# Layer 1 MLP with five deferred products and two weight sums on engines, two sums by DMA in layer 0

## The reference

```python
def _sq_relu_mlp(h, w1, w2):
    return jnp.square(jax.nn.relu(h @ w1)) @ w2
...
sh1, sc1, g1, sh2, sc2, g2 = jnp.split((silu_c @ ada_w[i] + ada_b[i])[:, None, :], 6, axis=-1)
...
h_lat = h_lat + g2 * _sq_relu_mlp(_modulate(_rms_norm(h_lat, norm2_g[i]), sh2, sc2), mlp_w1[i], mlp_w2[i])
```

## Time and profile before

| what | value |
|---|---|
| median of 3 runs | 2533.49 us |
| profiled execution | 2538.97 us |
| its span | 2537.4 us |
| TensorE matmul busy | 2310.9 us, 91% of the span |
| VectorE, ScalarE, GpSimd busy | 1748.4, 1148.5, 1150.7 us |
| mean granted TensorE clock | 0.960 of full speed |

### The profile page before, as it was taken

One profiled execution on the slowest core, in us unless ns is written; L12 is line 12 of the kernel. 1 busy time (PEld: TensorE's weight loads), 2 busy tenths in 40 slices (PEclk: granted clock), 3 DMA queues, 4 the chain that ended last, 5 costly groups with the idle time before them and its releaser, 6 DMA issues. The chain is left out here.

```text
span 2537.4 us, 38440 instructions
## 1 busy us (share of the span) xinstructions
PE 2310.9 (91%) x11430; PEld 1898.4 (75%) x11430; DVE 1748.4 (69%) x2843; ACT 1148.5 (45%) x2117; POOL 1150.7 (45%) x958
## 2 busy tenths in 40 slices
PE   5989989999999998999959979897988999999999
PEld 3768768788878787888848767775866777777777
DVE  5643886666666667666766478885378777787777
ACT  5544443333333333333344368886344545454554
POOL 0004533333433333334455657675644555465554
PEclk9999999999999999999969989999999999999999
DMA  7434325555555555444532211112311332322322
GB/s 267 166 133 166 101 54 145 148 153 137 144 135 143 140 147 136 132 132 132 141 111 83 100 57 34 34 44 113 112 46 46 100 95 91 91 91 87 99 87 95
DMA packets 132200, 283.55 MB, mean 112 GB/s; under 512 B 11408, under 2 KB 19984, under 8 KB 128784
## 3 DMA queue, kind: packets, MB, share of 16 engines
q1 hardware_dynamic: 111776, 242.09, 28.8%
q0 software_dynamic: 17408, 33.56, 7.9%
q10 hardware_dynamic: 2928, 6.82, 0.7%
HBM read 265.64 MB, written 83.89 MB: 138 GB/s over the span
## 5 line engine op out<-in xcount | busy, mean ns | idle before, releaser
L881 POOL TENSOR_TENSOR ht<-ht,l_side 128x512 f32<-128x512 f32 x112 | 147.6, 1318 | 401.1 <-ACT l_side L1020 397.2
L51 PE MATMUL l_z_ps<-nh,l_w1h 128*128 128x512 f32 (+1 forms) x816 | 292.9, 359 | 6.5 <-POOL l_w1l L58 3.4
L53 PE MATMUL l_z_ps<-nh,l_w1l 128*128 128x512 f32 (+1 forms) x816 | 291.7, 357 | 0.0
L52 PE MATMUL l_z_ps<-nl,l_w1h 128*128 128x512 f32 (+1 forms) x800 | 285.8, 357 | 0.0
L1324 DVE SCALAR_TENSOR_TENSOR ht<-l_yy_ps,mod,ht 128x512 f32<-128x512 f32 x336 | 236.4, 744 | 31.1 <-PE l_yy_ps L1640 29.9
L58 POOL TENSOR_TENSOR l_w1l<-early,l_w1h 128x512 fp32r<-128x512 f32 x104 | 136.4, 1318 | 190.0 <-ACT l_w1h L2189 190.0
L2754 PE MATMUL l_yy_ps<-l_ah,l_w2h 128*128 128x512 f32 x448 | 185.6, 414 | 22.2 <-DVE ht L2545 19.5
L1638 PE MATMUL l_yy_ps<-l_ah,l_w2h 128*128 128x512 f32 x448 | 191.2, 427 | 9.0 <-DVE ht L1324 9.0
L2081 POOL TENSOR_TENSOR ht<-ht,l_side 128x512 f32<-128x512 f32 x112 | 155.8, 1391 | 88.8 <-ACT l_side L2239 87.9
L3483 POOL TENSOR_TENSOR sc<-sc,den 128x640 f32<-128x640 f32 (+1 forms) x128 | 149.5, 1200 | 92.0 <-DVE den L3565 92.0
L1639 PE MATMUL l_yy_ps<-l_al,l_w2h 128*128 128x512 f32 x448 | 187.9, 420 | 0.0
(11 more groups left out here) (338 smaller groups left out, 6606.5 us busy)
## 6 DMA issues: line engine op xcount, KB each, us to landing
l_aw<-ada SPq DMA_DIRECT2D x128, 256.0 KB, 3.6
sums<-w SPq DMA_DIRECT2D x64, 512.0 KB, 7.4
maw<-ada SPq DMA_DIRECT2D x24, 1024.0 KB, 5.2
l_w1f<-w SPq DMA_DIRECT2D x32, 512.0 KB, 4.1
l_w2f<-w SPq DMA_DIRECT2D x32, 512.0 KB, 4.2
sums<-w POOLq DMA_DIRECT2D x32, 512.0 KB, 10.3
sums<-sums POOLq DMA_DIRECT2D x32, 512.0 KB, 6.1
l_w2f<-sums SPq DMA_DIRECT2D x64, 256.0 KB, 2.7
```

The lines of the kernel that those rows point to most:

```text
L51: pe.matmul(out, lh, rh, start=first, stop=False)
L52: pe.matmul(out, lh, rl, start=False, stop=False)
L53: return pe.matmul(out, ll, rh, start=False, stop=last)
```

## The change

In layer 0:

- `sums` keeps only S1 and S3 of w1 and w2. `start_sums` issues two copies a pair instead of four, and stands on SyncE's queue behind steps 2 to 7 instead of at the start of the pair. GpSimd issues two accumulating DMAs a pair instead of four (`add_sums`): one after M1's side add and the low parts behind it, the other at the end of the pair. Nothing is added on top of a sum any more.

In layer 1, from pair 2 on:

- S2 and S4 are formed in SBUF: for w1 by GpSimd (`sum1`, two additions a pair), for w2 by VectorE (`sum2`, two a pair). The loads of these four blocks go away (10 loads of 256 KB a pair instead of 14), the load slots and their order change.
- The low part of W2's S2 moves from VectorE to GpSimd, and the square of B21 from VectorE to ScalarE (`square_last`). B21's square now stands in an SBUF slot instead of PSUM, so M1 waits for the ReLU of B21, and M5 for the low part of T3.
- Five products are deferred instead of four. TensorE's order: M1, P2', M5, P3', M6, P4', M2, P5', M7, M3, P6', M4, P0, P1.
- The orders of ScalarE, VectorE, GpSimd and SyncE follow. Pairs 0 and 1 of layer 1, which use the plain product for the hidden layer, get the same sums for w2 and the new place of B21's square.

The diff, cut to its core:

```diff
-                    sp.dma_start(sums[0, 0:2, to]..., w1[1, one, :, :, 0:KC // 2]...).then_inc(s_sc, 16)
-                    sp.dma_start(sums[0, 2:4, to]..., w1[1, one, 0]...).then_inc(s_sc, 16)
-                    sp.dma_start(sums[1, 0:2, to]..., w2[1, two, :, :]...).then_inc(s_sc, 16)
-                    sp.dma_start(sums[1, 2:4, to]..., w2[1, chunks, :, 0:512]...).then_inc(s_sc, 16)
+                        sp.wait_ge(s_sums, p * 32)
+                    sp.dma_start(sums[0, :, to]..., w1[1, one, :, :, 0:KC // 2]...).then_inc(s_sc, 16)
+                    sp.dma_start(sums[1, :, to]..., w2[1, two, :, :]...).then_inc(s_sc, 16)
 
                 def pair(r, row, rows, first):
-                    if C:
-                        start_sums(r)
                     load1(r + 1, row(r + 1), 0)
                     if C and not first:
                         for k in range(2, STEPS):
                             load_a(r, row(r), k)
+                    if C:
+                        start_sums(r)
                     load1(r + 1, row(r + 1), 1)
...
                 def outputs(p, more):
-                    if C:
-                        if type(p) is not int or p:
-                            more_sums(p - 1, "S4")
-                        first_sums(p)
                     add(p, "M5")
...
                                 low1(p + 1, 1 if C else 0)
+                            if C:
+                                add_sums(p, 0)
...
                     if C:
-                        more_sums(p, "S2")
+                        add_sums(p, 1)
...
-                    more_sums(PAIRS - 1, "S4")
-                    pool.wait_ge(s_s4, 16 * PAIRS)
+                    pool.wait_ge(s_sums, 32 * PAIRS)
...
+                def sum1(p, i):
+                    a, b = (0, 1) if i == 2 else (2, 0)
+                    ...
+                    pool.tensor_tensor(w1f[:, a], w1f[:, a], w1f[:, b], ALU.add).then_inc(s_w1s, 1)
...
+                def square_last(p):
+                    act.wait_ge(s_rl, relu_at(p, "B21"))
+                    act.activation(inner("B21"), slot[RELU_SLOT["B21"]][:], ACT.Square).then_inc(s_sqa, 1)
...
                 def pair(p, earlier=True):    (VectorE)
                     if earlier:
                         pair_start(p)
-                    low2(p, 1)
-                    if earlier:
-                        acc(p - 1, 5)
-                    low2(p, 0)
                     zsum(p, "B11")
+                    if earlier:
+                        acc(p - 1, 5, (0,))
                     square(p, "B11")
+                    if earlier:
+                        acc(p - 1, 5, (1, 2, 3))
+                    low2(p, 0)
+                    sum2(p, 1)
                     zsum(p, "B22")
-                    low(p, "B11")
                     square(p, "B22")
                     zsum(p, "B12")
+                    if earlier:
+                        acc(p - 1, 6, (0,))
                     square(p, "B12")
+                    if earlier:
+                        acc(p - 1, 6, (1, 2, 3))
+                    low(p, "B11")
                     diff(p, "T1")
                     diff(p, "T2")
-                    if earlier:
-                        acc(p - 1, 6, (0, 1))
-                    square(p, "B21")
-                    if earlier:
-                        acc(p - 1, 6, (2, 3))
+                    diff(p, "T3")
                     low(p, "T2")
                     acc(p, 0, (0,))
-                    diff(p, "T3")
+                    low(p, "T3")
                     acc(p, 0, (1, 2, 3))
-                    low(p, "T3")
                     diff(p, "T4")
-                    acc(p, 1, (0, 1))
-                    low(p, "B21")
-                    acc(p, 1, (2, 3))
-                    low(p, "T4")
-                    acc(p, 2)
+                    acc(p, 1)
...
                 def pair(p, more, earlier=True):    (ScalarE)
...
+                    high(p, "B11")
+                    if earlier:
+                        side_read(p - 1, 6)
+                    high2(p, 2)
+                    high(p, "T2")
                     relu(p, "B21")
                     if more:
                         high1(p + 1, 0)
-                    high(p, "T2")
-                    if earlier:
-                        side_read(p - 1, 6)
+                    square_last(p)
                     high(p, "T3")
-                    high2(p, 2)
                     side_read(p, 0)
...
                 def pair(p, earlier=True):    (TensorE)
-                    for k, prod in enumerate(Z_ORDER):
+                    behind = {"M1": 2, "M5": 3, "M6": 4, "M2": 5, "M3": 6}
+                    for prod in Z_ORDER:
                         hidden(p, prod)
-                        if earlier and k < 3:
-                            product(p - 1, 3 + k)
-                    if earlier:
-                        product(p - 1, 6)
-                    for i in (0, 1, 2):
+                        if earlier and prod in behind:
+                            product(p - 1, behind[prod])
+                    for i in range(DEFERRED):
                         product(p, i)
```

More of the change, by code:

```diff
@@ L70, in sem @@
             return s
-        s_sums = [ctx.enter_context(nc.semaphore(n)) for n in ("sums13", "sums2", "sums4")]
+        s_sums = ctx.enter_context(nc.semaphore("sums"))
         def recycle_semaphores():
@@ L1891, in zsum_at, with after_square, summed1, summed2 @@
             return p * 3 + (PRE - 3 * PLAIN + ZSUMS.index(name) + 1)
-        def square_at(p, name):
-            order = Z_PLAIN[p] if is_plain(p) else SQUARES
-            return p * 4 + (PRE + order.index(name) + 1)
+        def after_square(eng, p, name):
+            if name == "B21":
+                eng.wait_ge(s_sqa, p + (PRE + 1))
+            else:
+                order = [n for n in Z_PLAIN[p] if n != "B21"] if is_plain(p) else SQUARES
+                eng.wait_ge(s_sqd, p * 3 + (PRE + order.index(name) + 1))
+        def summed1(eng, p, i):
+            eng.wait_ge(s_w1s, p * 2 + (PRE - 2 * PLAIN + W1_SUMS[i]))
+        def summed2(eng, p, i):
+            eng.wait_ge(s_w2s, p * 2 + (PRE + W2_SUMS[i]))
         def relu_at(p, name):
@@ L2174, in high1 @@
                 def high1(p, i):
-                    loaded1(act, p, i)
+                    if not is_plain(p) and i in W1_SUMS:
+                        summed1(act, p, i)
+                    else:
+                        loaded1(act, p, i)
                     if is_plain(p):
@@ L2228, in high @@
                             act.wait_ge(s_y, y_at(p - back, j, 3))
-                    if name == "B21":
-                        act.wait_ge(s_t, t_at(p, "T4"))
                     act.activation(operand(name)[0], inner(name), ACT.Copy).then_inc(s_ah, 1)
@@ L2348, in _ @@
                 relu(0, "B21")
+                square_last(0)
                 relu(0, "B12")
@@ L2409, in _ @@
                 pair(last, False)
+                side_read(last, 2)
                 high2(last, 6)
@@ L2558, in plain_rest @@
                     acc(p, 1, (0, 1))
+                    low(p, "T4")
+                    acc(p, 1, (2, 3))
                     low(p, "B21")
-                    acc(p, 1, (2, 3))
-                    low(p, "T4")
                     low(p, "T1")
@@ L2565, in plain_rest @@
                     low2(p, 6)
+                    sum2(p, 5)
                     acc(p, 3)
@@ L2579, in pair_start @@
                 def pair_start(p):
+                    low(p - 1, "T4")
+                    low(p - 1, "B21")
                     low(p - 1, "T1")
+                    acc(p - 1, 2)
+                    low(p - 1, "B22")
+                    low2(p - 1, 6)
+                    sum2(p - 1, 5)
                     acc(p - 1, 3)
-                    low2(p - 1, 6)
-                    low(p - 1, "B22")
                     low2(p - 1, 5)
@@ L2652, in _ @@
                 low(0, "B11")
-                square(0, "B21")
                 square(0, "B12")
-                diff(0, "T1")
                 square(0, "B22")
                 plain_rest(0)
-                low2(1, 1)
                 low2(1, 0)
+                sum2(1, 1)
                 square(1, "B11")
@@ L2804, in _ @@
                 pair(PAIRS - 1)
-                product(PAIRS - 1, 3)
+                for i in (2, 3):
+                    product(PAIRS - 1, i)
                 for n in range(3):
```

273 lines of the change are left out of this document (143 added, 130 removed).

## The result

| | median | runs | ratio to the kernel before | profiled execution | its span |
|---|---|---|---|---|---|
| before | 2533.56 us | 4 (2530.75 to 2535.92) | | 2538.97 us | 2537.4 us |
| after | 2434.24 us | 4 (2432.33 to 2434.94) | 0.9607, 95% interval 0.9591 to 0.9624 | 2434.44 us | 2432.9 us |

The median fell by 99 us, 3.9%; the forecast was 2428 with a range of 2408 to 2462. Between the spans of the two profiled executions the gain is 104.5 us, where the sum said 105.

The account below looks back on a forecast made before the run. TensorE was taken to bound both layers' MLPs, with layer 0 losing idle time and clock to late `ada_w` loads. Terms -90 - 5 - 6 - 6 + 2 = -105 from 2533.5 gave 2428 us, range 2408 to 2462.

Parts of the forecast that it names:

- The pauses: Layer 0's MLP pairs: all 14 TensorE stops before the last modulation step go, worth -90 us.
- (a): Sizing layer 0's pauses by pair length: 59.9 less 53.5 us, times 14 pairs, gives 90 us.
- (b): Sizing layer 0's pauses by 54.2 us idle plus 37 to 45 us of slow clock: 91 to 99 us.
- true control: Layer 0's last pair, copies behind the loads: VectorE waits only 0.63 us, steps 6 and 7 14.9 us after step 0.
- Last pair and tail: End of layer 0: late side adds in the last pair go, -5 us; one DMA fewer to await, -6 us.
- Layer 1, loop: Layer 1's 13 loop pairs: loss at bank read-outs falls from 1.5 to 1.0 us a pair, -6 us.
- Layer 1, outside the loop: Layer 1's pairs 0 and 1 and its very end: added sums on VectorE cost +2 us, bounds -2 and +5.
- VectorE and GpSimd on SBUF: Layer 1's new sums contend on shared SBUF interfaces: two `sum2` cost 2.4 us instead of 1.4, beside TensorE in the loop.
- (A): Rival, layer 0: pauses only shrink as accumulations run into the next pair's loads; +45 us, 2473; chance 9%.
- (B): Rival, layer 0: loads or VectorE's steps are late for another reason, so pauses stay; 2519 us; chance 3%.
- (C): Rival, layer 1: P1 waits longer as ScalarE and VectorE lock together; 2488 or 2448 us; chance above 2450 7%.
- (D): Rival, layer 1: GpSimd's 20 operations a pair set the pace; 2577 us at 2.5 us each; chance 2%.

Follow-up runs that it names:

- e2: The changed kernel with its two copies and two accumulations a pair put back at the old place at the pair's start: 2426.96 us, ratio 0.9559.
- e3: The kernel before with all four copies and four accumulating DMAs a pair at the new place, layer 1 as before: 2457.33 us, ratio 0.9692.
- e5: e2 with GpSimd issuing its two accumulations only after step 1 of the pair, so both lie beside the loads: 2452.74 us.
- e4: The kernel before with only layer 1's part of the change, layer 0 as before: 2537.2 us, ratio 1.0.
- e6: The changed kernel with GpSimd's wait for the last accumulations at layer 0's end moved to SyncE, ahead of layer 1's second-product weight loads: 2435.26 us.
- e7: The changed kernel with all VectorE read-outs of the first deferred product ahead of T3's low part in layer 1's pairs: 2420.23 us, ratio 0.9524.
- e9: The changed kernel run once more, unedited, in later rounds: 2434.85 us, ratio 0.9593.
- e1: The kernel before, unchanged, profiled a second time: median 2537.49 us, profiled execution 2537.39 us.

## Why the prediction was right, point by point

**The pauses (-90).** 91.8 measured, all 14 gone, pairs of 53.35 where 53.5 was worked out, the clock at 1.00, steps 6 and 7 14.9 us after step 0 (673.70 less 658.78). Both ways of sizing them held: (a), from pair lengths, to within 2 us, and (b), idle time plus slow clock, is 54.2 + 37.7 = 91.9 when the second part is taken from the matmuls' busy time. The last pair was a true control.

**What took them away.** The prediction names place and number together and read the earlier trace rows as three accumulations that happen to be issued there. e2, e3 and e5 correct this. Two sums at the old place have no pause, and two beside the loads have. The wait of 10.09 us in the first row made the place: it held S1 and S3 back into the time of the loads. The text had that number and used it only to say when S2 was issued. It had no effect on the forecast, as the pairs alone gain 75 us in e3 and 92 in e2, but it hid that the new place costs 6 us at the end.

**Last pair and tail (-5, -6).** 9.6 of 11. The tail was mis-sized by 1: the earlier trace rows have 6.1 us from S2's issue to S4's and 7.1 from there to the next stage; S2's wait is what goes, so 6.1 and not 7.1. Accordingly GpSimd's last issue to the next stage is 7.3 us, where 6 was said. This stretch also scatters by 2.5 us in the same code (64.1 and, in e4, 61.6). The forecast kept one DMA there as unavoidable; e2 shows it isn't, and e6 that taking the wait away doesn't help.

**Layer 1, loop (-6).** -4.2 over 12 pairs (0.34 a pair where 0.5 was said). The term that was mis-sized is the loss in P1: 1.07 us in place of 1.0, and 1.4 before in place of 1.5 (40.05 and 39.71 less 38.64). The mechanism was that of the text, and e7 shows that one moved line is worth three times what the deferral brought.

**Layer 1, outside the loop (+2, bounds -2 and +5).** It came out at +2, but by luck: both parts were wrong and cancel. From P1 of the last pair to the end it is +4.2 (34.3 less 30.1), where 1 to 2 was said for the end. Three low parts stand on VectorE ahead of the first read-out, two of them at 1.4 us. The first pairs, which were to lose a little, gained 2.2 in this trace, within their own scatter of 4. Also left out: B21's square now stands in SBUF, so the difference for T4 has both inputs there and takes 1641 ns in place of 678. It hides behind TensorE in the loop. Together layer 1 gave 2.1 of the 4 us; what is missing is the loop's. No timing here can tell 2.1 from nothing (e4). Its worth to this change is that it makes S2 and S4 unnecessary in layer 0.

**VectorE and GpSimd on SBUF.** The sums were priced at 1212 ns from the low parts; the two `sum2` have a mean of 1242 ns in the loop of the kernel after. That mean hides two durations. The group of the loop, and the two sums of one pair in order of time:

```profile
L2533 DVE TENSOR_TENSOR l_w2f<-l_w2f 128x512 f32<-128x512 f32 x20 | 24.8, 1242 | 0.3
```

```profile
1934.87 1.79 DVE L2533 TENSOR_TENSOR l_w2f<-l_w2f 128x512 f32<-128x512 f32 x1
...
1950.80 0.69 DVE L2533 TENSOR_TENSOR l_w2f<-l_w2f 128x512 f32<-128x512 f32 x1
```

The first starts while GpSimd adds (1934.26 to 1936.10), the second while GpSimd stands idle (1950.22 to 1952.24). Of the 31 sums from 1760 on in this trace the 14 that lie beside a GpSimd operation take 1.75 to 1.79 us, and the 17 that lie beside none 0.68 or 0.69. So the rule of the Trainium skill (GPSIMD Engine Reference, Key points: instructions with two SBUF inputs contend on the interface that GpSimd shares with VectorE) agrees with the trace for sums as well. The price reads as a wait and not as a slower rate: the slow sum ends 0.56 us after the GpSimd operation in which it began, and so does the difference for T4, at 1641 ns in the kernel after (1925.85 against 1925.29) and at 1037 in e7 (1922.70 against 1922.14), where it begins later within such an operation. GpSimd's own sum has a mean of 1284 ns in the loop.

**From the sum to the time.** The text took the median of three runs, 2533.5, and said that nothing depends on the 5.5 us to the profiled execution. All of the miss (2434.2 less 2428.5 is 5.7) lies in that sentence. The span of the profiled execution less the terms gives the time after (2538.97 - 105 = 2434), and in later rounds the kernel before had medians of 2538 to 2540, near its profiled execution; in the rounds of e9 the gain was 103 us. So the three runs were the untypical ones. Why is not known: the two prices of a pause do not explain it (e1).

**Luck in the sum.** That 104.5 met 105 so closely is in part luck. The pairs gave 2 us more than forecast and attention 1 that nobody forecast, the end of layer 0 gave 1.4 less and layer 1 2 less.

**Rivals.** (A), pauses that only shrink, is what e5 brings about, with 14.3 us of stops in 12 pairs; in the kernel after there is none. (B), loads late for another reason, falls, as all 14 stops went. (C), engines locked into each other in P1, did not come: the wait in P1 is 0.77 us, not 2.5, with no loss of clock. But its price at 2.5 us, without the lower clock, was probably set too low: all 28 stops in the pairs of before and e1, from 2.7 us on, were followed by the lower clock, and one of 1.7 us in e3. (D), GpSimd as the pace, needs 28 operations (39.7 / 1.42) and there are 20.

## What to carry to other kernels

When a transfer is late, look first for what delays the issue of its neighbours: a wait of an engine's queue for an earlier DMA moves all later ones. Here moving all the traffic gained 75 us in the pairs (e3), and removing half of it with its chain of waits 92 (e2). An engine that executes in order should take what frees a bank before what waits for another engine; one such line was worth 1.07 us in each of 14 pairs here. Where the terms of a sum are read from a profiled execution, take them off that execution's own time, and not off a median of few runs. A mean over a group can hide two durations, so look at the single rows before using it as a price.

## What the runs showed of the hardware

- A stop of TensorE in layer 0's pairs had three prices beyond its idle time: 0.3 us at most (nine of ten stops in e3, up to 1.6 us long), 1.8 us (stops of 2.7 to 4.25 us in e1, of 1.7 to 2.7 in e5), and 3.1 to 3.5 us (stops of 3.2 to 4.9 us in before and e1 and of 1.7 in e3).
- The end of a block holds GpSimd until its own DMA has landed, with or without a wait for it in the program (7.0 and 7.3 us behind the issue, 5.6 of them to the landing); without a DMA in flight it is 2.6 us behind the last operation.
- A VectorE sum with both inputs in SBUF took 0.68 or 0.69 us beside no GpSimd operation and 1.75 to 1.79 beside one. The difference for T4 in the same form took 701 to 1682 ns in the kernel after, by when in a GpSimd operation it began; with one input in PSUM it took 678 in all 12 pairs.
- A read-modify-write of 512 KB took 6.6 us as the median with one other beside it (e2), 7.9 in the kernel after and 10.3 for S1 and S3 in the kernel before. The 256 KB loads of `ada_w` went from 3.6 us as the median to 3.0 when half of the copies and accumulations went. In e3, with all of them at the new place, that median is 4.5, and yet the stops fell from 54.2 to 10.3 us: the median over all loads does not tell which of them TensorE will wait for.
